# Attention of a decoder layer: the eight query blocks of a head in the order 7, 0, 6, 1, 5, 2, 4, 3, and score matmuls of two blocks in one run

## What is computed

```python
q, k, v = parts of xn @ w_in
def block(q_blk, i):                      # 128 queries at a time, 8 blocks
    sc = einsum('bhcqd,bhckd->bhcqk', q_blk, k)          # c = 0, 1
    sc = where(k_pos <= q_pos, sc, -inf)                 # causal
    p = softmax(sc, axis=-1)
    p_diff = p[:, :, 0] - lam * p[:, :, 1]
    return einsum('bhqk,bhkv->bhqv', p_diff, v)
y_attn = rms_norm(o, subln_g) * (1.0 - lambda_init)
```

## Time and profile before

| | |
|---|---|
| median of 3 runs | 1766.31 us (1765.93 to 1766.45) |
| the profiled execution | 1766.17 us |
| its span in the trace | 1764.6 us |
| TensorE busy | 1754.1 us, 99% |
| VectorE busy | 1117.9 us, 63% |
| ScalarE busy | 738.1 us, 42% |
| GpSimd busy | 265.6 us, 15% |
| score matmuls (L2444) | 126.5 to about 470 us of the span, 576 of them |

### The profile page before, as it was taken

The page is one execution under the profiler, slowest core; times in us unless marked ns, Lnnn a source line. Parts: engine busy times, 40 slices in busy tenths (PEclk is TensorE's granted clock), DMA queues, the critical chain, the costliest instruction groups (busy, mean ns, idle before and its releaser), DMA issues.

```text
span 1764.6 us, 23983 instructions
## 1 busy us (share of the span) xinstructions
PE 1754.1 (99%) x8497; PEld 1455.0 (82%) x8497; DVE 1117.9 (63%) x1863; ACT 738.1 (42%) x1486; POOL 265.6 (15%) x555
## 2 busy tenths in 40 slices
PE   9999999999999999999999999999999999999998
PEld 7888888888888888888888888888888888888886
DVE  5327888888775764543565655776666655567676
ACT  5316666666743233343221123343333333344553
POOL 3322222222210001111100112101011000000011
PEclk9999999999999999999999999999999999999999
DMA  7421222222132223337635712223233322673443
GB/s 241 144 84 49 72 73 72 72 73 72 61 144 95 72 66 117 116 102 246 230 127 163 244 63 83 96 96 137 95 113 106 108 89 99 231 277 99 146 143 126
DMA packets 138047, 213.74 MB, mean 121 GB/s; under 512 B 7585, under 2 KB 94113, under 8 KB 136930
## 3 DMA queue, kind: packets, MB, share of 16 engines
q1 hardware_dynamic: 109200, 108.54, 19.5%
q0 software_dynamic: 28752, 103.98, 16.3%
q10 hardware_dynamic: 2, 0.00, 0.0%
HBM read 150.10 MB, written 62.39 MB: 120 GB/s over the span
## 4 chain that ended last, share of the span: by engine, by line
PE 99%; DVE 0%; ACT 0%; DMA 0%; issue 0%; POOL 0%; POOLq 0%; DVEq 0%; ACTq 0%
PE ps L2344 26%; PE ps L2679 22%; PE ps L2547 17%; PE ps L2735 12%; PE ps L2428 11%; PE ps L2444 3%; PE ps L2352 3%; PE ps L2466 3%; PE ps L2468 1%; DMA x_tile<-in_x_dram 0%; DVE d_op L1567 0%; ACT ps L1003 0%; DVE ring L1567 0%; POOLq L104 0%; DVE xs_tile L1598 0%
## 5 line engine op out<-in xcount | busy, mean ns | idle before, releaser
L2735 PE MATMUL ps<-d_op 128*128 128x512 f32 x924 | 210.3, 389 | 0.1
L2735 PEld LDWEIGHTS ps<-d_op 128*128 128x128 f32 x924 | 173.3, 188 | 36.8 <-DVE d_op L1567 0.5
L2679 PE MATMUL ps<-s_op,t_op_T 128*128 128x512 f32 x720 | 169.8, 389 | 0.0
L2428 PE MATMUL ps<-xn,ring 128*128 128x512 f32 x672 | 167.0, 398 | 0.3
L2679 PEld LDWEIGHTS ps<-s_op,t_op_T 128*128 128x128 f32 x720 | 135.2, 188 | 28.0
L2428 PEld LDWEIGHTS ps<-xn,ring 128*128 128x128 f32 x672 | 122.3, 188 | 26.0 <-issue 1.7
L2547 PE MATMUL ps<-s_op,x_op_T 128*128 128x512 f32 x576 | 135.9, 389 | 0.0
L2547 PEld LDWEIGHTS ps<-s_op,x_op_T 128*128 128x128 f32 x576 | 108.1, 188 | 22.4
L2679 PE MATMUL ps<-hn,t_op_B 128*128 128x512 f32 x480 | 115.1, 389 | 0.0
L2679 PEld LDWEIGHTS ps<-hn,t_op_B 128*128 128x128 f32 x480 | 90.1, 188 | 18.7
L1680 DVE CUSTOM_DVE_ANT_0 ps<-ps,mask 128x256 f32<-128x256 f32 (+7 forms) x128 | 94.4, 779 | 9.4 <-PE ps L2444 8.8
(11 more groups left out here) (269 smaller groups left out, 3366.3 us busy)
## 6 DMA issues: line engine op xcount, KB each, us to landing
pair<-in_w_gate_up_dram SPq DMA_DIRECT2D x20, 1024.0 KB, 5.1
rf_pieces<-s_scratch SPq DMA_DIRECT2D x74, 256.0 KB, 2.6
x_pair<-in_w_in_dram SPq DMA_DIRECT2D x16, 1024.0 KB, 6.7
raw<-in_w_in_dram SPq DMA_DIRECT2D x26, 512.0 KB, 4.0
s_scratch<-gated_ff POOLq DMA_DIRECT2D x40, 256.0 KB, 2.5
gate_in<-gate_scratch POOLq DMA_DIRECT2D x18, 512.0 KB, 3.5
v_scratch<-v_out POOLq DMA_DIRECT2D x32, 256.0 KB, 2.8
vh<-v_scratch POOLq DMA_DIRECT2D x16, 512.0 KB, 5.2
```

Source lines behind the costliest of these rows:

```text
L2428: last = pe.matmul(ps[:, proj_bank(first, half), :], proj_weights(which, par, a)[:, P * k:P * (k + 1)], xn[:, b, k, HALF * half:HALF * (ha ...
L2679: last = pe.matmul(ps[:, bank, :], t_op[name][:, a, k, :], block(b, k), start=opens and (k, a, b) == (0, HH, HH), stop=(k, a, b) == (3, LL ...
L2735: last = pe.matmul(ps[:, DOWN_BANKS[product][i], :], d_op[:, g % 4, a, P * i:P * (i + 1)], d_op[:, g % 4, 2 + b, :], start=opens and (a, b ...
```

## The change

Step i now handles block `BLOCK[i]`, with `BLOCK = (7, 0, 6, 1, 5, 2, 4, 3)`. Score runs stand in steps 0 (block 7), 1 (blocks 0 and 6), 3 (blocks 1 and 5), 5 (blocks 2 and 4) and 7 (block 3): five per head for six. A small block's scores lie at the end of the banks whose front part the large one of its pair uses, and VectorE waits with the small block for both blocks' scores. The first piece of projection ahead of the transposes in step 0 is gone. For q the second half of tokens is projected first. ScalarE's and VectorE's split of the k weights moves from step 2 to step 5; on VectorE it stands behind the projection's low part there. Head 7's last store waits as before, the others for one or more output transposes later.

```diff
+        BLOCK = (7, 0, 6, 1, 5, 2, 4, 3)
+        RUNS = {0: (0,), 1: (1, 2), 3: (3, 4), 5: (5, 6), 7: (7,)}
...
         def score_row(i, c):
-            first = 2 * c + (i % 2 if i < 4 else 0)
-            return ps[:, first:2 * c + 2, :].rearrange("p a b -> p (a b)")[:, 0:P * (i + 1)]
+            first = 2 * HALF - width(i) if i in (1, 3, 5) else 0
+            return ps[:, 2 * c:2 * c + 2, :].rearrange("p a b -> p (a b)")[:, first:first + width(i)]
+
+        def tokens_half(which, nth):
+
+            return 1 - nth if which else nth
...
-                    if i == 2 and not last:
+                    if i == 5 and not last:
                         split_weights(0, par)
...
                 if c == 0:
-                    dve.wait_ge(scores_done, t.at(1))
-                w = P * (i + 1)
+                    dve.wait_ge(scores_done, t.at(2 if i in (1, 3, 5) else 1))
+                w = width(i)
...
-                if i == 4:
-                    pe.wait_ge(proj_lo, p.at(-2))
-                if i >= 4 or i % 2 == 0:
-                    scores(par, i)
-                if i < 4 and i % 2 == 0:
-                    scores(par, i + 1)
-
-                ahead = 2 if i == 0 and not first else 0
-                if ahead:
-                    proj_part(0, 0, 1 - par, piece=(0, ahead))
+                if i == 1:
+                    pe.wait_ge(proj_lo, p.at())
+                for nth in RUNS.get(i, ()):
+                    scores(par, nth)
+
                 newer = (0, 0)
                 if not (first and i < 1):
                     before = (i - 1) % TT
                     diff_transposed(before)
-                    newer = (1, before // 4)
-                proj_part(i // 4, i % 4, 1 - par, piece=(ahead, 4), fresh=first and i == 0)
+                    newer = (1, BLOCK[before] // 4)
+                proj_part(i // 4, i % 4, 1 - par, fresh=first and i == 0, gates=gates)
```

More of the change, by code:

```diff
@@ L729, in norm, with store_y @@
                 t.next()
-            def store_y(par, h):
-                pool.wait_ge(tr_free[1], heads_out.at(1) * (TT + TT // 2) + TT)
+            def store_y(par, h, ahead=sum(m >= 4 for m in BLOCK[:3])):
+                pool.wait_ge(tr_free[1], heads_out.at(1) * (TT + TT // 2) + TT + ahead)
                 pool.dma_start(y_dram[bass.ds(h, 1)].rearrange("a p c -> (a p) c"),
@@ L759, in _ @@
             norm(7)
-            store_y(1, HEADS - 1)
+            store_y(1, HEADS - 1, ahead=0)
             pool.wait_ge(gates_first, 2)
@@ L1048, in proj_hi_of @@
                 act.wait_ge(proj_done, p.at(1))
-                copy((kt, qt)[which][:, par, HH, HALF * half:HALF * (half + 1)], ps[:, proj_bank(first, half), :],
+                at = HALF * tokens_half(which, half)
+                copy((kt, qt)[which][:, par, HH, at:at + HALF], ps[:, proj_bank(first, half), :],
                      scale=(1.0, HD ** -0.5)[which]).then_inc(proj_hi, 1)
@@ L1117, in y_hi @@
                 act.wait_ge(tr_done[1], tr[1].at(1))
-                copy(y_out[:, par, HH, P * i:P * (i + 1)], ps[:, TB[1], 0:P], scale=g_sub[:, :])\
+                copy(y_out[:, par, HH, P * BLOCK[i]:P * (BLOCK[i] + 1)], ps[:, TB[1], 0:P], scale=g_sub[:, :])\
                     .then_inc(tr_hi, 1)
@@ L1127, in step_of @@
                     before = (i - 1) % TT
-                    for b in range(before // 4 + 1):
-                        blocks = min(4, before + 1 - 4 * b)
+                    for b, blocks in groups_of(before):
                         transposed_hi(b, pt[:, before % 2, HH, 4 * b:4 * b + blocks, :], blocks)
@@ L1654, in proj_lo_of @@
                 dve.wait_ge(proj_hi, p.at(1))
-                buf, s = (kt, qt)[which], slice(HALF * half, HALF * (half + 1))
+                at = HALF * tokens_half(which, half)
+                buf, s = (kt, qt)[which], slice(at, at + HALF)
                 dve.scalar_tensor_tensor(buf[:, par, LL, s], ps[:, proj_bank(first, half), :], (1.0, HD ** -0.5)[which],
@@ L1713, in step_of @@
                 if not lag:
-                    if i == 2 and not last:
-                        split_weights(0, par)
                     if i == 6 and last:
@@ L1721, in step_of @@
                         split_weights(1, par)
+                    if i == 5 and not last:
+                        split_weights(0, par)
                 if lag < 3 and not (first and i < 2):
@@ L2416, in _, with proj_part @@
             heads_v = Count()
-            def proj_part(which, part, par, first=False, piece=(0, 4), fresh=False):
+            def proj_part(which, part, par, first=False, piece=(0, 4), fresh=False, gates=False):
                 half, k0 = part // 2, 4 * (part % 2)
+                tokens = half if gates else tokens_half(which, half)
                 if part == 0 and piece[0] == 0:
@@ L2438, in scores @@
                 wait_for(pe, exp_done, t.at() * 2)
-                for chunk in range(i // 4 + 1):
-                    w = min(HALF, P * (i + 1) - HALF * chunk)
+                m = BLOCK[i]
+                for chunk in range(m // 4 + 1):
+                    w = min(HALF, width(i) - HALF * chunk)
                     for n_pass, (a, b) in enumerate(PASSES):
@@ L2443, in scores @@
                             rows = slice(HD * c, HD * (c + 1))
-                            last = pe.matmul(score_row(i, c)[:, HALF * chunk:HALF * chunk + w], qt[rows, par, a, P * i:P * (i + 1)],
+                            last = pe.matmul(score_row(i, c)[:, HALF * chunk:HALF * chunk + w],
+                                             qt[rows, par, a, P * m:P * (m + 1)],
                                              kt[rows, par, b, HALF * chunk:HALF * chunk + w],
@@ L2450, in diff_transposed @@
                 pe.wait_ge(diff_ready, t.at())
-                for b in range(i // 4 + 1):
-                    blocks = min(4, i + 1 - 4 * b)
+                for b, blocks in groups_of(i):
                     transpose_rows(b, e_t[:, i % 2, 0, HALF * b:HALF * b + P * blocks], blocks)
@@ L2515, in _ @@
             for i in range(TT):
-                step_of(1, i)
+                step_of(1, i, gates=True)
             r.next(2 * HEADS + 2)
```

25 lines of the change are left out of this document (15 added, 10 removed).

## The result

The changed kernel takes **1783.91 us** (median of 4 runs, 1783.58 to 1784.28); the kernel before took 1766.38 us beside it (4 runs, 1765.93 to 1766.62). The ratio is 1.0100 with a 95% interval of 1.0082 to 1.0117, the difference 17.5 us. The forecast was 1783.3 us, slower.

The account below looks back on a forecast made before the run. TensorE was taken as the bound. Heads 1 to 6 +13.3 us, head 0 +3.3 and head 7 +0.4 make +17.0 on 1766.3: 1783.3 us, range 1779.5 to 1787, extended to 1790 on the upper side.

Parts of the forecast that it names:

- What bounds, and where: TensorE, 99% busy, bounds the kernel; a change pays only where it takes work, gaps or waits from TensorE.
- Time to free the bank: Projection bank, last matmul to end of VectorE's subtraction: 1.35 us taken, upper bound 2.27 us.
- Rival 1: ScalarE and VectorE free the bank late in steps 1, 3, 5: +16.6 us, about 1800 us; chance 0.07.
- Restart after the subtraction: TensorE's projection goes on 0.15 us after VectorE's subtraction frees the bank.
- Softmax of the large blocks: TensorE waits for the differences of blocks 6 and 4: 0.3 us for both, bounds 0 and 0.6.
- Rival 2: Large blocks' softmax is the longer chain, two differences 0.5 us later in seven heads: +7, 1790 us; chance 0.10.
- What is saved: One score run less, 0.36 us, and step 0's split projection gone, 0.1 us: 0.45 to 0.5 us a head.
- Heads 0 and 7: First and last head, reckoned apart from heads 1 to 6: +3.3 us for head 0, +0.4 for head 7.
- The range: 1779.5 to 1787 us from small waits (2 us), savings (1 us) and new waits (1.8 us); upper side extended to 1790.
- The clock: TensorE's granted clock should stay at the 2.4 GHz level despite waits of 0.6 to 1.6 us three times a head.
- rival 3: Clock falls: a tenth of the attention's 350 us at 1.2 GHz adds 17 us or more, 1800 and above; chance 0.04.
- Rival 4: Bank is free within the smallest cover, 0.43 us, so only savings remain: 6.4 us gained, 1760 us; chance 0.03.

Follow-up runs that it names:

- run 1: Changed kernel, with VectorE's subtraction that ends the freeing of the projection bank covering 256 of its 512 columns from head 1 on; 1778.40 us.
- run 2: Changed kernel with the same order of blocks but one score run in every step, eight a head; 1778.25 us.
- run 4: Changed kernel with block 3 first, pairs in steps 2, 4, 6, q's first half first and weight splits in steps 2 and 6; 1765.57 us.
- run 5: Kernel before, with the scores of blocks 0 and 1 in two runs, one score run more a head; 1768.56 us.
- run 6: Kernel before, without the first 6 projection matmuls ahead of block 7's transposes in step 0; 1768.81 us.

## Why the prediction was right, point by point

- *What bounds, and where.* Right: TensorE's stream decides, and the change acts through the cover between two halves of the projection. Runs 1, 2 and 4 each move that cover or that chain, and the time follows.
- *Time to free the bank*, two bounds 1.35 and 2.27 us, the lower taken. Right: 1.35 us in steps 1, 3 and 5. Rival 1 (both engines late) is out by the rows of steps 1 to 5 above.
- *Restart after the subtraction*, 0.15 us everywhere. Mis-sized in two places of three: 0.06 us in steps 2 and 6 (231.95 to 232.01, 255.15 to 255.21), 0.15 only in step 4 (243.67 to 243.82), the very place from which the figure was read. That makes the waits 0.55 for 0.64 and 0.80 for 0.89; step 4 is 1.22 for 1.23. Sum 2.57 for 2.76.
- *Softmax of the large blocks*, 0.3 us taken (0 to 0.6). Right: 0.29. Rival 2 is out at this size, but run 2 shows how near it is: with a shorter run in step 1 it comes to 0.71 us. The forecast gave block 7's difference about a microsecond to spare in the changed kernel; it has 0.6.
- *What is saved.* The term was 0.45 to 0.5 us a head. By the period: 2.57 + 0.29 - 0.34 - 2.16 = 0.36 us. By runs 5 and 6: 0.25 for the run and 0.13 for the split, 0.38. Run 2 prices a run at 0.34. So a run has no single price, 0.25 to 0.34 as it was measured; the balance of the changed kernel, 0.36 less 0.13 for the split, puts the one that is saved at 0.23, against 0.36 in the forecast. The split was guessed well. Over- and underestimate (waits 0.19 less, savings 0.12 to 0.14 less) nearly cancel in a head, 2.16 for 2.2, and that is luck.
- *Heads 0 and 7*, 3.7 us; measured 4.2. Head 0's waits were 1.17 (1.1), 1.55 (1.63), 1.30 (1.35) and 0.79 us (0.89). Head 7 has gate waits of 0, 0.50 and 0.06 us, and 0.52 us at 489.92 that the forecast had only as "perhaps 0.3": block 4's last transpose waits for the second bank (L1710 in the waits view). With the 13.0 us of the six middle heads that makes 17.2 us.
- *The range.* Its own terms (2, 1 and 1.8 us) added to 1783.3 give 1780.3 to 1788.1 and not 1779.5 to 1787; the measured time lies in either.
- *The clock.* In the changed kernel the granted clock is 1.00 in every window of the attention, so rival 3 did not occur. The Trainium skill (TensorE: Matmul & The Clock Gate, A second HAM failure mode: psum-queue depth-cycling) warns of swings; the changed kernel's trace does not show one with 21 waits of 0.5 to 1.55 us for the bank. A single fall in run 2's trace, behind waits that are not for the bank, is told in the last section.
- *Rival 4* would have needed a bank that is free in 0.43 us. Run 4 shows the other way to it: not a faster bank, but the cover put where the bank is needed.

## What to carry to other kernels

When one accumulator bank is used again and again, write down for each reuse what stands between the last matmul of the old half and the first of the new (the cover), and beside it the chain that empties the bank; the sum of the shortfalls is the price, and it is paid however "busy" the engine looks. An order that saves a whole run can lose more by taking that run out of such a gap; the same runs one step later gave the loss back (1765.6 us for 1783.9), and 4.3 us more once the last wait was filled as well. And before a wait is filled, name its instruction by its size in the timeline: a cure one step away from it does harm.

## What the runs showed of the hardware

Inside the attention the clock fell in one of the twelve traces, in head 0 of run 2. (Several traces, that of the kernel before among them, also show it below 1.00 in the last 8 us of the span, far behind the attention.) The windows of run 2 (granted clock third from the end) and its timeline:

```profile
132.00:134.00 2.00, 0.55 (x6) 0.44 (x6) 1.68 (x4) 0.21 (x2) 0.00 (x0) 1.00 0.03 8
134.00:136.00 2.00, 1.90 (x11) 1.72 (x12) 1.14 (x6) 1.21 (x3) 0.00 (x0) 0.83 0.00 0
136.00:138.00 2.00, 2.00 (x6) 1.58 (x5) 1.40 (x5) 1.52 (x5) 0.00 (x0) 0.50 0.00 0
138.00:140.00 2.00, 2.00 (x9) 1.35 (x10) 0.00 (x0) 0.43 (x1) 0.00 (x0) 0.81 0.00 0
```
```profile
132.36 0.55 PE L2461 MATMUL ps<-kt,qt 64*128 64x128 f32 x6 [1.10 <-ACT e_t L1105]
134.10 1.09 PE L2367 MATMUL ps<-ident,e_t 128*128 128x128 f32 x8 [1.19 <-DVE e_t L1687]
...
136.90 0.63 PE L2444 MATMUL ps<-xn,k_other_lo 128*128 128x512 f32 x1
137.32 1.06 PE L2444 MATMUL ps<-xn,k_other_hi 128*128 128x512 f32 x2
```

Two waits of 1.17 us (for exponentials) and 1.24 us (for a difference), from start to start, stood there with only six small score matmuls between them. Behind them the granted clock is 0.50, the 1.2 GHz level, and the projection's matmuls start 0.43 us apart (136.90, 137.32) in place of 0.23, from 135.6 to 138.6; seven of them cost 0.2 us more each and two a part of that, 1.6 us. All four runs of that kernel have a mean clock of 0.998 for 0.999. In the changed kernel head 0 has waits of 1.17 and 1.55 us, but a score run of 18 matmuls and a whole projection part between them, and no fall. So the fall that rival 3 feared does occur in a kernel whose step 1 has a shorter run, and it cost 1.6 us where it came once. That the two waits are its cause was not tested by a run of its own.

The restart latency of TensorE behind a semaphore differs by place: 0.06 us behind VectorE's subtraction in steps 2 and 6, 0.15 us in step 4, where a second wait, for the weights, stands beside it. That the second wait is the cause was not tested.
